# Prompt chunks of an mLSTM placed between the halves of the last eighteen projection tiles of a hybrid recurrent decoder step

## What is computed

```
z = rms_norm(x) @ w_in               # q k v o-gate (4 x 512 columns) | gates | 14 x 128 RWKV columns
for each chunk:                      # b, m_t: running sums and maxima of the gate rows
    w   = exp(b_t - b_s + i_s - m_t) where s <= t
    qk  = (q @ k.T) * w
    num = s_inter * (C @ q) + qk @ v
    den = s_inter * (n . q) + sum(qk)
    h   = num / max(|den|, exp(-m_t))
    C, n = dec * C + sum(wl * v k.T), dec * n + sum(wl * k)
y_m = sigmoid(o) * layer_norm(h)
```

## Time and profile before

| | us |
|---|---|
| three timed runs | 1763.88, 1765.21, 1765.22 |
| median | 1765.21 |
| span of the profiled execution (no other time of it is given) | 1763.6 |
| end of the last projection matrix multiplication of `e_in`, from the span's start | 231.15 |
| start of `rwkv_prep` on DVE | 326.13 |
| end of `rwkv_prep` on DVE | 353.19 |

### The profile page before, as it was taken

How to read it: one execution, slowest core, us unless ns; L and a number is a source line. 1 busy time by engine, 2 the same in 40 slices (tenths; PEclk the granted TensorE clock), 3 DMA queues, 4 the chain that set the end, 5 groups by cost and what they waited for, 6 DMA issues and landing times. The chain is left out here.

```text
span 1763.6 us, 35383 instructions
## 1 busy us (share of the span) xinstructions
PE 1634.1 (93%) x14910; PEld 1576.0 (89%) x14910; DVE 1053.1 (60%) x1533; ACT 471.8 (27%) x688; POOL 875.7 (50%) x731
## 2 busy tenths in 40 slices
PE   6999996588998999999989998999899999998996
PEld 5999985487987999999989998977799999998996
DVE  4816768747645777776632239676676777765012
ACT  4002123610133343333310031132414333332001
POOL 4666688094013644444376656700374444445763
PEclk8999988688999999999999999998999999999998
DMA  4222111021052222222222222274332222222222
GB/s 176 84 71 83 60 74 54 1 75 56 13 200 69 90 84 83 83 83 83 72 66 88 76 79 60 71 210 139 91 98 77 84 83 83 84 83 61 81 83 88
DMA packets 50679, 149.09 MB, mean 85 GB/s; under 512 B 17552, under 2 KB 19232, under 8 KB 48416
## 3 DMA queue, kind: packets, MB, share of 16 engines
q1 hardware_dynamic: 50592, 147.91, 26.3%
HBM read 127.58 MB, written 19.13 MB: 83 GB/s over the span
## 5 line engine op out<-in xcount | busy, mean ns | idle before, releaser
L280 PE MATMUL PP<-arena_r,dual_r 128*128 128x288 f32 (+1 forms) x6428 | 1116.9, 298 | 39.9 <-POOL dual_r L267 16.2
L280 PEld LDWEIGHTS PP<-arena_r,dual_r 128*128 128x128 f32 (+1 forms) x6428 | 965.3, 190 | 44.3 <-POOL dual_r L267 13.9
L280 PE MATMUL PP<-hT_r,dual_r 128*128 128x288 f32 (+1 forms) x2176 | 647.7, 298 | 0.0
L267 POOL TENSOR_TENSOR dual_r<-w_ring,dual_r 128x1024 fp32r<-128x1024 f32 (+1 forms) x198 | 485.1, 2450 | 17.7 <-ACT dual_r L1962 4.6
L267 POOL TENSOR_TENSOR dual_r<-w_ring,cst 128x1024 fp32r<-128x1024 f32 (+1 forms) x114 | 216.7, 1901 | 408.6 <-PE PP L280 262.2
L280 PEld LDWEIGHTS PP<-hT_r,dual_r 128*128 128x128 f32 (+1 forms) x2176 | 410.5, 189 | 1.3
L270 DVE SCALAR_TENSOR_TENSOR rowbuf<-rowbuf,convp 128x592 f32<-128x592 f32 x176 | 271.3, 1542 | 91.3 <-ACT rowbuf L1985 90.7
L280 PE MATMUL PP<-arena 64*64 64x64 f32 (+6 forms) x3640 | 206.0, 256 | 37.1 <-DVE arena L267 15.3
L280 PEld LDWEIGHTS PP<-arena 64*64 64x64 f32 (+2 forms) x3640 | 182.8, 148 | 57.9 <-issue 32.6
L1962 ACT ACTIVATE dual_r<-w_ring 128x1024 fp32r<-128x1024 f32 x84 | 89.2, 1062 | 332.1 <-PE PP L280 332.1
L267 DVE TENSOR_TENSOR xT<-PP,xT 128x576 f32<-128x576 f32 x32 | 24.2, 758 | 255.5 <-PE PP L280 255.5
(11 more groups left out here) (266 smaller groups left out, 1348.9 us busy)
## 6 DMA issues: line engine op xcount, KB each, us to landing
w_ring<-in_w SPq DMA_DIRECT2D x150, 512.0 KB, 3.5
w_ring<-in_w_down SPq DMA_DIRECT2D x32, 448.0 KB, 3.3
w_ring<-in_w_down SPq DMA_DIRECT2D x16, 512.0 KB, 3.5
xT<-in_x SPq DMA_DIRECT2D x8, 576.0 KB, 7.1
gy_scratch<-dual SPq DMA_DIRECT2D x1, 2304.0 KB, 7.0
dual<-gy_scratch SPq DMA_DIRECT2D x1, 2304.0 KB, 13.7
out_y<-hT SPq DMA_DIRECT2D x4, 576.0 KB
xT<-in_C SPq DMA_DIRECT2D x1, 2064.0 KB, 9.2
```

The lines of the kernel that those rows point to most:

```text
L267: return eng.tensor_tensor(out, a, b, op)
L280: return nc.tensor.matmul(out, lhsT, rhs, start=start, stop=stop)
```

## The change

The four prompt chunks and the scores and tokens of the sample chunk move from behind the projection into its last eighteen tiles, 12 to 29 (`E_LEAD` = 12). PE runs tiles 12 to 29 out of a loop and places chunk c's work between tile halves: scores ahead of tile 12 + 4c, tokens between the halves of tile 13 + 4c, the outputs of heads 0 and 1 between the halves of tile 14 + 4c, those of heads 2 and 3 in tile 15 + 4c. Only the sample chunk's outputs stay behind the projection. The chunks use banks 4 to 7 alone, heads 0 and 2 sharing bank 6 and heads 1 and 3 bank 7; `mlstm_columns` moves ahead of tile 12. DVE and ACT take their chunk work after the tile of the same number. The o-gate's sigmoids move to tiles 16 to 19 on ACT, SP issues the load of the sample states C ahead of that of the S5 inputs, `num2`, `vaug` and `ktok` get other memory, and POOL's `s5_phases` also waits for the last prompt chunk's variances.

```
+        def nd(c, h, k, n=P):
+            return bank((6, 7, 6, 7)[h] if c < NCH else (6, 7, 2, 3)[h])[0:n, 129 * k:129 * k + 129]
...
             pool.wait_ge(S("proj_done"), E_TILES)
+            pool.wait_ge(S("hn_var"), NCH)
...
+            def ml_tokens(c):
+                n, cols = span(c)
+                pe.wait_ge(S("ml_att"), c + 1)
+                for h in range(MH):
+                    nc.tensor.transpose(bank(4)[0:n, h * P:(h + 1) * P], zm[:, 8 + h, cols], ident)
+                for h in range(MH):
+                    last = nc.tensor.transpose(bank(5)[0:n, h * P:(h + 1) * P], zm[:, 4 + h, cols], ident)
+                last.then_inc(S("ml_tok"), 1)
...
+            def e_in():
+                project("e_in", n=E_LEAD)
+                mlstm_columns()
+                for u in range(2 * (E_TILES - E_LEAD)):
+                    j, a = E_LEAD + u // 2, u % 2
+                    s, c = j % 2, u // 8
+                    if u % 8 == 0:
+                        ml_scores(c)
+                    if u % 8 == 3:
+                        ml_tokens(c)
+                    if u % 8 == 5 and c < NCH:
+                        ml_outputs(c, (0, 1))
+                    if u % 8 == 7 and c < NCH:
+                        ml_outputs(c, (2, 3))
+                    if a == 0:
+                        pe.wait_ge(S("w_split"), j + 1)
+                        pe.wait_ge(FREE[s], j // 2 + 1)
+                    last = half("e_in", s, a)
+                    if a == 1:
+                        last.then_inc(S("proj_done"), 1)
...
             def mlstm():
...
                 for s in range(2):
                     pe.wait_ge(FREE[s], USE["e_out"] // 2 + 1)
...
+                ml_outputs(NCH, range(MH))
...
-            project("e_in", None, {11: mlstm_columns})
+            e_in()
...
+            for j in range(E_LEAD - 1, E_TILES):
...
+                if (j + 1 - E_LEAD) % 4 == 0:
+                    ml_exp(c)
+                    if c:
+                        ml_square(c - 1)
+                if (j + 1 - E_LEAD) % 4 == 1:
+                    ml_vtok(c)
+                if c < NCH and (j + 1 - E_LEAD) % 4 == 2:
+                    ml_num(c, (0, 1))
+                if c < NCH and (j + 1 - E_LEAD) % 4 == 3:
+                    ml_num(c, (2, 3))
+                if 16 <= j < 20:
+                    o_gate(j - 4)
...
+                for j in range(E_LEAD - 1, E_TILES):
+                    if j >= E_LEAD:
+                        tile(j)
+                    c, part = (j + 1 - E_LEAD) // 4, (j + 1 - E_LEAD) % 4
+                    if part == 0:
+                        ml_decay(c)
+                        if c:
+                            ml_norms(c - 1)
+                        ml_weights(c)
+                    if part == 1:
+                        if c < NCH:
+                            ml_keys(c)
+                        if c:
+                            ml_variances(c - 1)
+                    if c < NCH and part == 2:
+                        ml_outputs(c, (0, 1))
+                    if c < NCH and part == 3:
+                        ml_outputs(c, (2, 3))
                 shift(13)
...
             def mlstm():
...
                 chain(V.memset(qm, 0.0))
...
+                ml_keys(NCH)
+                ml_outputs(NCH, range(MH))
                 dve.wait_ge(S("rw_kkn"), 1)
```

More of the change, by code:

```diff
@@ L1481, in project, with half @@
                         between()
[L1482 to L1495, removed]
+                with pe.Fori(1, n // 2) as i:
+                    for s in range(2):
+                        pe.wait_ge(S("w_split"), 2 * i + (CHUNK0[name] + s + 1))
+                        pe.wait_ge(FREE[s], i + (USE[name] // 2 + 1))
+                        for a in range(2):
+                            last = half(name, s, a)
+                        last.then_inc(S("proj_done"), 1)
+            def half(name, s, a):
+                h = slice(a * TH, (a + 1) * TH)
+                for k in range(KT):
+                    c = slice(k * P, (k + 1) * P)
+                    last = mm3(PP[s][:, a, 0:TH], w_hi[:, s, c], w_lo[:, s, c],
+                               H_HI[name][k][:, h], H_LO[name][k][:, h], k == 0, k == KT - 1)
+                return last
             def down(l):
@@ L1555, in mlstm_back @@
                 last.then_inc(S("ml_back"), 1)
-            def mlstm():
[L1558 to L1600, removed]
@@ L2007, in _ @@
             A(t_s, l_st, ACT.Exp).then_inc(S("s5_trig"), 1)
+            act.wait_ge(S("ml_rows"), 1)
+            for r in (r_s, r_w, r_dec[:, 0:12]):
+                A(r, r, ACT.Exp).then_inc(S("ml_exps"), 1)
+            A(r_e, r_m, ACT.Exp, scale=-1.0).then_inc(S("ml_exps"), 1)
             act.wait_ge(S("o_rows"), 1)
@@ L2011, in _ @@
             A(t_c, t_c, ACT.Sin).then_inc(S("s5_trig"), 1)
[L2012 to L2030, removed]
             def ml_exp(c):
@@ L2411, in e_in @@
                     S("ad_copied"), 1)
-                for j in range(16):
+                for j in range(E_LEAD):
                     evac("e_in", j, zm[:, j, :], MHD ** -0.5 if 4 <= j < 8 else None)
@@ L2441, in shift, with tile @@
                     V.tensor_copy(shout[:, k, 1:9], samples(e[:, 1:])[:, :, 8]).then_inc(S(f"ext_free{s}"), 1)
-                for k in range(14):
+                def tile(j):
+                    if j < 16:
+                        evac("e_in", j, zm[:, j, :])
+                        return
+                    k = j - 16
                     s = k % 2
@@ new lines, in ml_keys @@
+            def ml_keys(c):
+                dve.wait_ge(S("ml_tok"), c + 1)
+                if c < NCH:
+                    kp = bank(5).rearrange("p (h n) -> p h n", h=4)
+                    tt(V, ktok, kp, bc(wlc[:, c, :], 2, 128), ALU.mult).then_inc(S("ml_tokc"), 1)
+                    return
+                dst = qm.rearrange("p h (j x) -> p h j x", x=72)[:, :, :, 0:8]
+                V.tensor_copy(dst, zm[:, 0:4, SEQ:T].rearrange("p h (j n) -> p h j n", j=8)).then_inc(
+                    S("ml_tokc"), 1)
+                kp = bank(5)[0:NSAMP].rearrange("p (h n) -> p h n", h=4)
+                chain(tt(V, wlm[0:64, :, 0:4], bc(wlc[0:64, c, :], 2, 4), bc(seqhalf, 1, 4), ALU.mult))
+                for h in range(MH):
+                    last = tt(V, Km[:, h], bc(kp[:, h, :], 1, 4), bc(wlm[0:64, h, 0:4], 2, 128), ALU.mult)
+                last.then_inc(S("e_samples"), 1)
@@ new lines, in ml_outputs @@
+            def ml_outputs(c, hs):
+                n = L if c < NCH else NSAMP
+                for h in hs:
+                    dve.wait_ge(S("ml_na"), 4 * c + h + 1)
+                    x = num(c)[0:n, h, :]
+                    ins = tt(V, x, x, nd(c, h, 0, n), ALU.add)
+                    if c < NCH:
+                        ins = stt(Cst[:, h, :], Cst[:, h, :], decb[:, h, c:c + 1], nd(c, h, 2), ALU.mult, ALU.add)
+                        ins.then_inc(S("ml_state"), 1)
+                    else:
+                        if h == MH - 1:
+                            ins.then_inc(S("ml_outc"), 1)
+                        ins = tt(V, Cs[:, h], Cs[:, h], bc(decb[:, h, NCH:NCH + 8], 2, 129), ALU.mult)
+                        if h == MH - 1:
+                            chain(ins)
@@ L2535, in back @@
                        zm[:, 12:16, cols], ALU.mult).then_inc(S("ycat"), 1)
-                V.memset(vaug[:, :, 128:129], 1.0)
-                V.memset(Cst, 0.0)
-                dve.wait_ge(S("ml_exps"), 5)
-                decay(0)
-                weights(0)
-                keys(0)
-                chain(V.memset(qm, 0.0))
-                for c in range(NCH):
-                    decay(c + 1)
-                    outputs(c)
-                    weights(c + 1)
-                    keys(c + 1)
-                    if c:
-                        variances(c - 1)
-                    norms(c)
-                variances(NCH - 1)
-                outputs(NCH)
+                chain(V.memset(qm, 0.0))
+                ml_keys(NCH)
+                ml_outputs(NCH, range(MH))
                 dve.wait_ge(S("rw_kkn"), 1)
```

229 lines of the change are left out of this document (116 added, 113 removed).

## The result

The changed kernel takes 1768.76 us (median of 20 runs, 1764.75 to 1774.19), the kernel before, measured beside it, 1765.69 (20 runs, 1758.53 to 1770.03). The ratio is 1.0021 with a 95% interval of 1.0011 to 1.0031: slower by some 3.7 us by the ratio (the medians differ by 3.1), where the prediction had it 3.1 us faster. The profiled execution has a span of 1766.7 us, 3.1 above that of before.

The account below looks back on a forecast made before the run. Bound: PE's projection up to 231.15 us, then DVE's chain that sets the RWKV recurrence's start. Preparation starts 11.6 us earlier, the collision costs 8.5, leaving 3.1: 1763.6 - 3.1 = 1760.5, with 1.6 added 1762.1 us; range 1752 to 1769.

Parts of the forecast that it names:

- the 350.1 that was worked out: End of the preparation of the RWKV recurrence: start at 314.5 plus 27.1 plus 8.5 us, 3.1 us earlier than before.
- The end of the projection: Last projection product on PE: 32.0 us later than before, at 263.1, from chunks, sample work, column wait and joins.
- what was said of the moved DVE and ACT work: Chunk work on DVE and ACT during the projection: costs nothing, DVE keeping over 4 us of room in four tiles.
- the rival in which DVE becomes the bound: Projection: norms wait for POOL's split, PE waits 4.8 us in three chunks, 14.4 in all, 1776.5 us; chance 0.1.
- The rival: Clock in the projection: five groups of 4-row products lose 1.2 us each, 6 us in all, 1768.1 us; chance 0.15.
- the forecast for each of chunks 1 to 3: Projection on PE, tokens of one chunk to the next: 4 x 6.36 + 6.89 = 32.33 us.
- the wait for the columns: Ahead of tile 12: PE waits for DVE to copy the result of `mlstm_columns`, taken as 1.2 us, bounds 0 to 4.6.
- the joins: Projection on PE: switches between the two kinds of product at some 17 places, taken as 0.5 us in all.
- From there to `kkrow`: Projection end to `kkrow`: 5.4 + 9.1 + 2.0 + 4.05 = 20.5 us, `kkrow` at 283.6, now waiting for PE.
- From `kkrow` to the preparation: Stretch from `kkrow` to the preparation's start: 30.9 us, unchanged from before, so the preparation starts at 314.5.
- The collision: Preparation: five 1024-wide POOL instructions of the S5 tables make DVE wait 1.7 us each, 8.5 us in all.
- The case of the upper bound: Preparation, if the tables run behind: six wide POOL instructions at 1.9 us and four narrower ones, 19 us.

Follow-up runs that it names:

- 3: Changed kernel with the decay products reading 128 rows, 124 of them zeros, instead of 4: 1760.43 us, ratio 0.9979 to the kernel before.
- 5: Changed kernel with the 4-row decay products split into two groups of four, half a tile apart: 1766.88 us, ratio 1.0024 to the kernel before.
- experiment 7: Changed kernel with S5 turns behind POOL's splits and 128-row decay products, but the table phases held until `kkrow` is made: 1756.87 us, ratio 0.9960.
- 6: Changed kernel with S5 turns behind POOL's splits, 128-row decay products, and columns made by fifteen 128-row transposes: 1746.87 us, ratio 0.9914.
- 9: The same kernel as 6, measured again beside the same kernel as 8: 1742.19 us, ratio 0.9880 to the kernel before.
- 1: Changed kernel with POOL's S5 turns done in pieces behind its splits of tiles 12 to 29: 1755.86 us, ratio 0.9944 to the kernel before.
- 2: Kernel before with POOL's S5 turns done in pieces behind its splits of tiles 10 to 29: 1760.93 us, ratio 0.9986 to the kernel before.
- experiment 4: Changed kernel with both S5 turns behind POOL's splits and 128-row decay products: 1746.47 us, ratio 0.9894 to the kernel before.
- 8: The same kernel as experiment 4, measured again beside two other kernels: 1750.25 us, ratio 0.9924 to the kernel before.

## Why the prediction was wrong

The preparation ended at 359.6, 9.5 us after the 350.1 that was worked out; then 3.3 us came back. Step by step:

**The end of the projection: 268.5, not 263.1.** No row of PE waits for DVE, ACT or POOL but the 0.5 us for the columns, so what was said of the moved DVE and ACT work was right, and the rival in which DVE becomes the bound did not occur. What failed is the choice of the full clock for the moved products. The rival named it, at 1.2 us for each of five groups; measured is 33.60 - 32.33 = 1.3 above the forecast for each of chunks 1 to 3, no drop at the sample's group, and what is left of the 5.4, some 1.6, around the first group (net of the 0.7 by which the wait for the columns was set too high, and of the 0.5 for the joins, which the 33.60 holds already). The drop itself costs more than the rival's 1.2: the two windows behind chunk 1 lack 0.44 and 0.41 of 2 us each, 1.7 us. At full clock a chunk would thus take some 0.4 less than the 32.33 worked out, which hid part of it. Experiments 3 and 5 show that it is the products of 4 rows, eight together: with 128 rows, or in groups of four, the clock stays at 2.4 GHz. The argument against the rival, that these products are 2 of the 3.1 us of a group with full products on both sides, did not hold. That its 1768.1 us is near the measured time is chance: it left out the larger collision, and what follows from 280 us on. Of the Trainium skill ("TensorE: Matmul & The Clock Gate", Loop structure matters more than you think) the rule that dense products without waits keep the clock up was cited for it; here the trace disagrees, with PE busy for 2.00 of 2.00 us at a granted clock of 0.56, and the measurement decides.

**From there to `kkrow`: 21.0 us, predicted 20.5.** Right, and the wait is for PE, as said.

**From `kkrow` to the preparation: 27.5 us, not the 30.9 that was carried over.** This part gave 3.4 us. The granted clock from 280 to 300 us was 0.88; with early turns it was 0.80, and the same part took 30.4. Why the clock was higher here was not tried; in the other versions with all chunks in the projection this part takes 29.5 to 30.4 us.

**The collision: 15.5 us, not 8.5.** The mechanism was right, and the price of 1.7 us for a wide instruction too (1.7 with 1024 columns in experiment 7, 1.4 in the mixture of 512 and 1024), though the row it was taken from has a product that takes 1.22 us alone and not the 1.34 worked out. The term was mis-sized in its count, eleven instead of five, because POOL was forecast too early. The phases began at 298.33, not at 287.7: half of the 10.6 us came with the projection's end, the other half from the turns, which took 40.5 us and not the 35.2 of before. They ran beside the four sample outputs' products of 128 x 1032, and the wait goes both ways: a POOL instruction of 0.25 us took 1.48 when DVE had such a product running, and four such waits make 4.6 of the 5.3 us. The case of the upper bound, with all six and four narrower ones, had the count nearly right (ten); its 19 us are too high, since it priced the narrower ones like the wide. The Trainium skill ("SBUF — State Buffer", Who interferes with whom) has the shared port pair held for a whole instruction, and this the traces bear out: one late DVE instruction for each wide POOL instruction. By it six instructions of 1.90 and five of the 1.06 that 512 columns take alone would hold DVE for 16.7 us, an estimate; measured were 15.1.

**Behind the preparation: 3.3 us given back,** which no step had. The first 10 us of the recurrence, after the change and then before:

```profile
359.60:369.60 10.00, 7.83 (x146) 7.45 (x148) 4.42 (x12) 0.98 (x2) 9.39 (x9) 0.81 0.90 307
```

```profile
353.20:363.20 10.00, 7.78 (x106) 7.43 (x108) 3.38 (x8) 0.98 (x2) 9.37 (x9) 0.50 0.91 301
```

The granted clock is 0.81 where before it was 0.50, with 146 products done instead of 106. It is not the stretched preparation that brings this: the same windows show 0.79 to 0.80 in experiments 3, 6 and 9 and 0.50 to 0.54 in 1, 2, 4, 5, 7 and 8, and of the kernels with a stretched preparation 3 is in the first list, 5 and 7 in the second. A kernel that was traced twice fell on the same side both times (4 and 8 with 0.50 and 0.54, 6 and 9 with 0.79), but of the others there is one trace each. What decides it stays open.

The sum: 350.1 + 5.4 + 0.5 - 3.4 + 7.0 = 359.6, and 1760.5 + 9.5 - 3.3 = 1766.7 us, the measured span. That the miss is not twice as large is luck: the 3.4 and 3.3 us that came back were in no step. Moving the chunks itself does what it says: without the two side effects (experiment 4) it is 14 to 17 us faster than before, and the kernel before with early turns only 2.7 (by the medians). Padded decay products were not tried in the kernel before.

## What to carry to other kernels

When work moves into an earlier stage, all background work of another engine that starts at that stage's end moves later too: work out where its widest instructions land against the critical two-input DVE instructions, counting its own waits for DVE. Check small products that are put among dense ones for the granted clock behind them, since the wait table shows nothing; rows of zeros kept it up here and made the group shorter (2.59 us in place of 2.96). A move that loses a little may hide a gain that a second, cheap move sets free.

## What the runs showed of the hardware

Eight products of 4 rows and 128 columns, 2 us in a dense stream, took the granted clock from 1.00 to 0.56 and 0.59 in the two stretches of 2 us behind them; four of them did not, nor did eight of 128 rows of which 124 are zero, nor eight of 4 rows and 64 columns. DVE holds POOL as POOL holds DVE: 0.25 us became 1.48 beside a product of 128 x 1032. The way from 4-row products to full ones costs PE time at full clock too: from the start of the last pair of 4-row products to that of the second full product behind it the changed kernel takes 0.55 us (188.31 to 188.86), with 128 rows 0.35 (184.21 to 184.56), part of the 32.44 against 31.67 us for a chunk in experiments 5 and 3. And one and the same stage, the start of the recurrence, ran at 0.50 to 0.54 of the full clock in seven traces and at 0.79 to 0.81 in four; between the kernels before and after this moves the end by some 3 us without a change in that stage.
